# A hybrid decoder layer in one kernel: memory tiles turned later, waits per tile, and sample values in two reduced-precision parts

## The reference

```
x = x + o @ w_out                                  # end of the mixing stage
h = rmsnorm(x, g_xattn)
m = rmsnorm(mem_prompt, g_mem)                     # 256 memory tokens
k, v = m @ xa_w_k, m @ xa_w_v                      # for the prompt; both are outputs too
q = h @ xa_w_q                                     # 4 heads of 512
prompt:  p = softmax(q k^T / sqrt(512)) over 256 memory tokens;  o = p v
samples: the same with cache_mem_k, cache_mem_v    # a K and a V of 256 x 512 for each of 8 samples x 4 heads
x = x + o @ xa_w_o
h = rmsnorm(x, g_ffn)
x = x + (silu(h @ ffn_w_gate) * (h @ ffn_w_up)) @ ffn_w_down
y = rmsnorm(x, g_final)
```

## Time and profile before

| | |
|---|---|
| median of 3 runs | 1907.69 us (1902.86 to 1907.97) |
| the profiled execution's own time | 1903.32 us |
| its span (first to last instruction) | 1901.6 us |
| mean granted TensorE clock, as a share of full | 0.988 |
| PE busy | 1841.4 us, 97% |
| DVE, ACT, POOL busy | 60%, 41%, 10% |

### The profile page before, as it was taken

The page is one execution under the profiler, slowest core; times in us unless marked ns, Lnnn a source line. Parts: engine busy times, 40 slices in busy tenths (PEclk is TensorE's granted clock), DMA queues, the critical chain, the costliest instruction groups (busy, mean ns, idle before and its releaser), DMA issues.

```text
span 1901.6 us, 34195 instructions
## 1 busy us (share of the span) xinstructions
PE 1841.4 (97%) x13832; PEld 1736.7 (91%) x13832; DVE 1141.9 (60%) x1569; ACT 774.5 (41%) x797; POOL 182.0 (10%) x172
## 2 busy tenths in 40 slices
PE   7999999989999899999999999999999999999996
PEld 5999999987999899888648999999999999999996
DVE  4888447744776567555455656666544566665444
ACT  4554545342353343444442344444333344433332
POOL 1000000002105400000002520000000000000331
PEclk9999999999999999999999999999999999999998
DMA  7555545442235557887683668887455889984552
GB/s 214 178 175 175 177 139 170 144 137 99 89 110 186 192 182 244 283 300 249 233 285 112 204 197 252 247 246 217 135 178 179 249 244 249 251 227 136 182 181 76
DMA packets 414225, 367.08 MB, mean 193 GB/s; under 512 B 11391, under 2 KB 373886, under 8 KB 413334
## 3 DMA queue, kind: packets, MB, share of 16 engines
q1 hardware_dynamic: 386456, 340.69, 58.2%
q10 hardware_dynamic: 27694, 25.33, 4.2%
HBM read 347.84 MB, written 18.35 MB: 193 GB/s over the span
## 4 chain that ended last, share of the span: by engine, by line
PE 90%; DVE 5%; ACT 2%; issue 1%; DMA 0%; DVEq 0%; POOL 0%; ACTq 0%; POOLq 0%
PE ps L458 63%; PE ps L534 9%; PE ps L515 4%; DVE w_lo L439 2%; PE ps L936 2%; PE ps L1405 2%; PE ps L501 1%; PE ps L1217 1%; PE ps L1413 1%; PE ps L1232 1%; ACT w_hi L432 1%; PE ps L1135 1%; PE ps L1063 1%; PE ps L1374 1%; PE ps L1143 1%
## 5 line engine op out<-in xcount | busy, mean ns | idle before, releaser
L432 ACT ACTIVATE w_hi<-raw 128x2048 fp32r<-128x2048 f32 (+1 forms) x285 | 512.2, 1797 | 906.9 <-PE ps L458 731.8
L439 DVE TENSOR_TENSOR w_lo<-raw,w_hi 128x2048 fp32r<-128x2048 f32 (+1 forms) x285 | 617.8, 2168 | 289.5 <-ACT w_hi L432 286.6
L458 PE MATMUL ps<-act_hi,w_lo 128*128 128x264 f32 x2560 | 734.3, 287 | 5.7 <-DVE w_lo L439 3.6
L458 PE MATMUL ps<-act_lo,w_hi 128*128 128x264 f32 x2560 | 726.7, 284 | 0.0
L458 PE MATMUL ps<-act_hi,w_hi 128*128 128x264 f32 x2560 | 726.3, 284 | 0.0
L458 PEld LDWEIGHTS ps<-act_hi,w_lo 128*128 128x128 f32 x2560 | 483.8, 189 | 9.6 <-DVE w_lo L439 3.6
L458 PEld LDWEIGHTS ps<-act_lo,w_hi 128*128 128x128 f32 x2560 | 484.0, 189 | 0.4
L458 PEld LDWEIGHTS ps<-act_hi,w_hi 128*128 128x128 f32 x2560 | 481.4, 188 | 0.0
L458 PE MATMUL ps<-ff_hi,w_lo 128*128 128x264 f32 x704 | 200.3, 285 | 0.0
L458 PE MATMUL ps<-ff_hi,w_hi 128*128 128x264 f32 x704 | 200.0, 284 | 0.0
L458 PE MATMUL ps<-ff_lo,w_hi 128*128 128x264 f32 x704 | 199.4, 283 | 0.0
(11 more groups left out here) (417 smaller groups left out, 2155.6 us busy)
## 6 DMA issues: line engine op xcount, KB each, us to landing
raw<-in_w_in_dram SPq DMA_DIRECT2D x56, 1024.0 KB, 7.5
raw<-in_ffn_w_gate_dram SPq DMA_DIRECT2D x44, 1024.0 KB, 5.8
raw<-in_ffn_w_up_dram SPq DMA_DIRECT2D x44, 1024.0 KB, 5.9
raw<-in_ffn_w_down_dram SPq DMA_DIRECT2D x32, 768.0 KB, 4.8
raw<-in_ffn_w_down_dram SPq DMA_DIRECT2D x32, 640.0 KB, 6.0
raw<-in_w_out_dram SPq DMA_DIRECT2D x16, 1024.0 KB, 6.2
raw<-in_xa_w_q_dram SPq DMA_DIRECT2D x16, 1024.0 KB, 7.3
raw<-in_xa_w_k_dram SPq DMA_DIRECT2D x16, 1024.0 KB, 6.9
```

Of the source, the lines that this page charges most:

```text
L432: act.activation(w_part(ph, w_hi[b]), raw_part(ph, r, half), ACT.Copy)\
L439: dve.tensor_tensor(w_part(ph, w_lo[b]), raw_part(ph, r, half), w_part(ph, w_hi[b]), ALU.subtract)\
L458: mm = pe.matmul(ps[:, acc(ph, u), 0:ph.cols], w[b][:, k, :], v[:, kk + k, 0:ph.cols], start=first and k == 0 and m == 0, stop=last and k ...
```

## The change

It has four parts. (1) POOL copies the first two `mt` slices ahead of `squares(2)`, and TensorE does x_q's unit 0 ahead of the first turn. (2) `products` gets a callback before each weight tile; at x_q's and gu0's unit 0 it waits for tiles 13, 14, 15 of `act` one by one, and the waits for all tiles ahead of gu0 and gu1 are gone. (3) Values 0 to 17 are summed by TensorE as two fp32r matmuls (rounded part and remainder): ACT writes the rounded part (`high_values`), DVE the remainder (`low_values`). (4) The split of x_o's second unit comes after value 19 and 20 on ACT and DVE, `keep_rows(3, 1)` after values 16 and 17, and the samples' rows are turned and split one step earlier, with x_o's first unit waiting for the last prompt step only at its last weight tile.

```diff
+HALVED = 18
...
+            pool.wait_ge(mrows_landed, 16)
+            for b in range(2):
+                W(pool, "m_turned", b + 1)
+                pool.tensor_copy(mt[b], mrows[:, :, b * P:(b + 1) * P]).then_inc(mt_ready, 1)
             squares(2, taken(PH["w_out"]), x, TT)
...
-            pool.wait_ge(mrows_landed, 16)
-            with pool.Fori(0, KT // 2) as i:
+            with pool.Fori(1, KT // 2) as i:
...
                 b, h = n // XH, n % XH
-                pe.wait_ge(v_mixed, n + 1)
                 at = NB * XH - 1 - (NB * h + b)
-                pe.matmul(ps[0:NB * XH, 6, :], window[:, at:at + NB * XH], piece_at(NB * XH + n)[0][:, 0, :],
+                if n < HALVED:
+                    pe.wait_ge(v_mixed, n + 1)
+                    r = ring_r[(NB * XH + n - EARLY_PIECES) % RING]
+                    pe.matmul(ps[0:NB * XH, 6, :], window[:, at:at + NB * XH], r[:, 0, :], start=n == 0, stop=False)
+                    pe.matmul(ps[0:NB * XH, 6, :], window[:, at:at + NB * XH], r[:, 1, :], start=False, stop=False)\
+                      .then_inc(N["s_o"], 1)
+                    return
+                pe.wait_ge(v_summed, n + 1)
...
+            def x_taken_to(ph):
+                def ready(k):
+                    if k >= 13:
+                        pe.wait_ge(acc_free, ph.t0 - KT + k + 1 + ACC_CREDIT)
+                return ready
             for n in range(3 * KT):
                 if n < KT:
+                    if n == 0:
+                        products(pe, ph, i, u, act_hi, act_lo, ready=x_taken_to(ph))
                     pe.wait_ge(m_taken, n + 1)
                     pe.wait_ge(mt_ready, n + 1)
...
-                    products(pe, ph, i, u, act_hi, act_lo)
                     if n == 0:
                         sum_squares(2, TT)
+                    else:
+                        products(pe, ph, i, u, act_hi, act_lo)
...
             for j in range(KT):
+                if j == KT - 1:
+                    pe.wait_ge(rows_copied, 3)
+                    for d in range(4):
+                        mm = turn(ps[:, 7, d * 32:(d + 1) * 32], orow[:, d * P:(d + 1) * P])
+                    mm.then_inc(rows_turned, 1)
                 prompt_values(j)
...
-                pe.wait_ge(acc_free, ph.t0 + ACC_CREDIT)
                 for u in range(4):
-                    products(pe, ph, 0, u, act_hi, act_lo)
+                    products(pe, ph, 0, u, act_hi, act_lo, ready=x_taken_to(ph) if half == 0 and u == 0 else None)
...
+            def high_values(n):
+                act.wait_ge(v_summed, n + 1)
+                r = (NB * XH + n - EARLY_PIECES) % RING
+                act.activation(ring_r[r][:, 1, :], ring[r][:, 0, :], ACT.Copy).then_inc(v_halved, 1)
...
+            def low_values(n):
+                dve.wait_ge(v_halved, n + 1)
+                r = (NB * XH + n - EARLY_PIECES) % RING
+                dve.tensor_tensor(ring_r[r][:, 0, :], ring[r][:, 0, :], ring_r[r][:, 1, :], ALU.subtract).then_inc(v_mixed, 1)
...
             for n in range(3 * KT):
-                split(*unit_at(n + 2))
+                if n < 3 * KT - 1:
+                    split(*unit_at(n + 2))
...
                         first_values(2 * (n - 39) + v)
+                    for v in range(2):
+                        high_values(2 * (n - 39) + v)
+                if n == 3 * KT - 1:
+                    keep_rows(3, 1)
             for v in range(18, NB * XH):
+                if v == 20:
+                    split(*unit_at(3 * KT + 1))
                 first_values(v)
...
                 if j < 14:
                     second_values(18 + j)
+                if j == 2:
+                    split(*unit_at(3 * KT + 1))
+                if j == KT - 1:
+                    dve.wait_ge(rows_turned, 1)
```

More of the change, by code:

```diff
@@ L126, in build @@
         rstd = place("rstd", [P, TT], F32)
+        SQ0 = Here.at
         sq = place("sq", [P, 2, TT], F32)
@@ L251, in build @@
         p_s = sq[0:NB * XH, 1, 0:NM]
-        window = sq[:, 0, 5 * NB * XH:7 * NB * XH - 1]
+        window = place("window", [P, 2 * NB * XH - 1], R32, SQ0 + 20 * NB * XH)
+        ring_r = [place(f"ring_r{b}", [P, 2, XD], R32, A0 + 4096 * b) for b in range(RING)]
         orow = place("orow", [NB * XH, XD], F32, Q0 + 4 * KT * TT + 4 * (KT // XH * NM - XD))
@@ L317, in build @@
         v_mixed = sem("v_mixed")
+        v_halved = sem("v_halved")
+        v_summed = sem("v_summed")
         rows_copied = sem("rows_copied")
@@ L443, in mixed_unit, with products @@
             return PH["r" if n < 8 else "z"], n % 8 // 4, n % 4
-        def products(pe, ph, i, u, hi, lo, k0=0, middle=None):
+        def products(pe, ph, i, u, hi, lo, k0=0, middle=None, ready=None):
             b, n = (ph.u0 + u) % 2, ph.u0 + 4 * i + u
@@ L456, in products @@
             for k in range(ph.k):
+                if ready is not None:
+                    ready(k)
                 for m, (w, v) in enumerate(((w_lo, hi), (w_hi, lo), (w_hi, hi))):
@@ L565, in build @@
                      "gdn_sq gdn_sum gdn_ln gdn_normed gdn_turned gdn_ktok gdn_vb gdn_g gdn_gcol gdn_scal "
[L566 removed]
+                     "gdn_pair gdn_dmin gdn_dexp gdn_lt gdn_qkm y_done y_copied tyuy_done inv_ready "
                      "gdn_kbg gdn_f gdn_e gdn_out half_hi half_lo half_done o_mixed bst_landed gdn_sx gdn_sbc gdn_sval "
@@ L926, in _ @@
                     pool.tensor_copy(mt[b], mrows[:, :, ds(i * 2 * P + b * P, P)]).then_inc(mt_ready, 1)
-            pool_link(pool, pool.memset(window, 0.0))
-            pool.memset(window[:, NB * XH - 1:NB * XH], 1.0).then_inc(columns_ready, 1)
+            pool_link(pool, pool.memset(window[:, :].bitcast(F32), 0.0))
+            pool.memset(window[:, NB * XH - 1:NB * XH].bitcast(F32), 1.0).then_inc(columns_ready, 1)
             squares(3, taken(PH["x_o"]), x, TT)
@@ L1402, in sample_values @@
                 b, h = n // XH, n % XH
-                pe.wait_ge(v_mixed, n + 1)
                 at = NB * XH - 1 - (NB * h + b)
-                pe.matmul(ps[0:NB * XH, 6, :], window[:, at:at + NB * XH], piece_at(NB * XH + n)[0][:, 0, :],
+                if n < HALVED:
[6 more added lines that the diff above has]
+                pe.wait_ge(v_summed, n + 1)
+                pe.matmul(ps[0:NB * XH, 6, :], window[:, at:at + NB * XH].bitcast(F32), piece_at(NB * XH + n)[0][:, 0, :],
                           start=n == 0, stop=n == NB * XH - 1).then_inc(N["s_o"], 1)
@@ L1459, in _, with values_kept @@
                     sample_values(18 + j)
-            pe.wait_ge(rows_copied, 3)
-            for d in range(4):
-                mm = turn(ps[:, 7, d * 32:(d + 1) * 32], orow[:, d * P:(d + 1) * P])
-            mm.then_inc(rows_turned, 1)
+            def values_kept(k):
+                if k == KT - 1:
+                    W(pe, "att_oe", KT)
             W(pe, "s_oe", 1)
-            phase_pe(pe, PH["x_o"], ow_hi, ow_lo)
+            ph = PH["x_o"]
+            for u in range(4):
+                products(pe, ph, 0, u, ow_hi, ow_lo, ready=values_kept if u == 0 else None)
+            with pe.Fori(1, ph.loops) as i:
+                for u in range(4):
+                    products(pe, ph, i, u, ow_hi, ow_lo)
             for half in range(2):
                 ph = PH[f"gu{half}"]
-                pe.wait_ge(acc_free, ph.t0 + ACC_CREDIT)
                 for u in range(4):
-                    products(pe, ph, 0, u, act_hi, act_lo)
+                    products(pe, ph, 0, u, act_hi, act_lo, ready=x_taken_to(ph) if half == 0 and u == 0 else None)
                     if half == 0 and u == 0:
@@ L1906, in _ @@
                     keep_columns((n - 20) // 4)
-                if n >= KT and n % 4 == 3:
+                if n >= KT and n % 4 == 3 and n < 3 * KT - 1:
                     keep_rows(n % KT // 4, n // (2 * KT))
@@ L2487, in _ @@
                     dve.tensor_scalar(p_s, p_s, small[0:32, REC, 12:13], None, ALU.mult).then_inc(N["s_pn"], 1)
-                if n:
+                if 0 < n < 3 * KT - 1:
                     split(*unit_at(n + 2))
@@ L2502, in _, with by_head @@
                         second_values(2 * (n - 39) + v)
+                    for v in range(2):
+                        low_values(2 * (n - 39) + v)
+            def by_head(v):
+                return v.rearrange("p (h d) b -> p h d b", d=4)
             for j in range(KT):
@@ L2505, in _ @@
                     second_values(18 + j)
+                if j == 2:
+                    split(*unit_at(3 * KT + 1))
+                if j == KT - 1:
+                    dve.wait_ge(rows_turned, 1)
+                    src = ps[:, 7, 0:KT * NB].rearrange("p (d h b) -> p h d b", d=4, h=XH)
+                    link(dve.tensor_copy(by_head(ow_hi[:, :, T:TT]), src))
+                    dve.tensor_tensor(by_head(ow_lo[:, :, T:TT]), src, by_head(ow_hi[:, :, T:TT]), ALU.subtract)\
+                       .then_inc(N["s_oe"], 1)
                 W(dve, "att_o", j + 1)
```

9 lines of the change are left out of this document (1 added, 8 removed).

## The result

The changed kernel took 1884.44 us (median of 4 runs, 1881.83 to 1889.15), the kernel before 1905.28 in the same comparison (4 runs, 1902.18 to 1907.97): a ratio of 0.9894, 95% interval 0.9863 to 0.9924, a gain of about 20 us, between 14.5 and 26. The forecast was 1888, within 1883 to 1896. The profiled execution took 1886.84, its span 1885.1, at a mean clock of 0.990.

The account below looks back on a forecast made before the run. TensorE, busy 97% of the span, bounds the kernel. Gains 6.5 + 5.2 + 2.8 + 1.0 + 1.6 + 0.3 = 17.4 give 1885.9 from the profiled run, 1890.3 from the median; forecast 1888, range 1883 to 1896.

Parts of the forecast that it names:

- x_q's start: Between w_out and x_q: POOL's part and the turn leave the way, first unit 6.07 instead of 7.28; gain 6.5 us.
- Values 0 to 15: Until unit 47 ends: two fp32r matmuls per value cut each group from 7.61 to 6.71; gain 5.2 us.
- PE never idle for more than 0.1: Expected sign in the after profile, 920 to 970 us: groups of 6.7 without longer PE idles.
- the one that the prediction charged to unit 40: PE waits behind unit 40, which has no values ahead and ends before the 7.1 chain; 0.2 us deducted.
- Values 16, 17 and the prompt's values with x_o's start: Behind unit 47: 2.8 us net from values and prompt steps, plus 1.0 from x_o starting earlier.
- the return of the postponed split: In the prompt's loop: the split delays value 21 some 1.6 and values 18 and 19 another 0.3; cost 2.0 us.
- gu0, gu1: At both starts: gu0's 1.4 wait for `act_lo` goes, gain 1.6 us; gu1's 0.7 wait shrinks, gain 0.3.
- The value chain: Rival, chance 0.15: the values' chain through ACT and DVE outlasts its lead and lengthens groups; 1891 to 1898 us.
- the clock rival: Rival, chance 0.15: short idles at the values' end drop the clock there too; 1890 to 1891.5 us.
- The slower rival: Rival, chance 0.02: `high_values` waiting for DVE block ACT's next `w_hi`, so units hang on it; 1911 us or more.

Follow-up runs that it names:

- The three kernels without this part: Kernel before with only POOL's tiles copied early, only x_q's unit 0 ahead of the turn, or only values 0 to 17 halved: 1896.22, 1895.42, 1896.85 us.
- The doubled copies: Changed kernel with ACT's copy of each value's high half issued twice in the groups behind units 39 to 47: 1897.8 us, one run.
- the kernel with the values first: Changed kernel with the values' operations on ACT and DVE issued ahead of the same unit's weight split and eviction: 1881.7 us, ratio to before 0.9896.
- 32 values halved: Changed kernel with values 18 to 31 also split into two fp32r parts, in the prompt's loop: 1893.9 us, one run.

## Why the prediction was right

**x_q's start** (6.5, measured 6.53). The start 0.06 behind `act_lo`, the unit of 6.07 and the full clock came as read from gu0, and the turn took 0.22 for the 0.25. (The 0.5 from which the 0.25 was halved is in no row: to the unit's first record before it is 0.32, to its row in the chain 0.67.) What the prediction did not see is that either of the two edits would do.

**Values 0 to 15** (5.2, measured 5.5). The matmul with 32 columns costs 0.233, as taken. The chain was sized at 7.1 and measured 7.10, its added operations 0.65 and 0.68 for 0.67 and 0.60. The mis-sized term is PE's own group, 6.71 forecast and 6.51 measured: the 5.78 of a unit behind a float32 value holds 0.2 that a unit behind reduced-precision matmuls (5.58) does not. So PE was 0.2 faster a group, and then the chain, which had just fitted in, took 0.16 of that back: 6.67 on average. The 0.04 that is left, six times, is the 0.3 between 5.2 and 5.5. "PE never idle for more than 0.1" was wrong by this: it idles 0.3 in every second group. The wait of 0.96 ahead of value 0 is the one that the prediction charged to unit 40.

**Values 16, 17 and the prompt's values with x_o's start** (2.8 + 1.0, measured 4.6). The idles came where forecast and slightly smaller: 1.41 for 1.6 and 1.21 for 1.5, 0.20 for 0.3. The end of unit 47 to the first prompt step took 3.5 instead of the 3.8, which is 0.3 of the difference. The mis-sized term is the return of the postponed split, 2.0 in the sum: from the first prompt step to value 31 the loop took 29.07, where it took 28.10 with 0.56 of slow clock in it, 1.5 more at the same clock, and moving the split out of the loop won 1.3. x_o's start came as taken: value 31 to x_o's first matmul took 4.74 before and takes 3.60, a gain of 1.1 for the 1.0, and x_o starts 0.07 behind the prompt's last step.

**gu0, gu1** (1.6 and 0.3, measured 1.7 and 0.25). The three kernels without this part take 887.7 to 888.2 from x_o's start to the end, the kernel before 887.9, the changed one 885.6: 2.2. All kernels that have this part lie at 885.6 to 886.2; but all of them also have x_o's first unit started early, so no run shows this part by itself.

**The rivals.** The value chain did take over, but by 0.3 in every second group, not by the 0.5 in each that the rival stood for. (That 0.5 was itself too high: with both added operations at 0.9, the steps of the prediction give 5.0 + 3 x 0.9 = 7.7, so d is 0.6 and a group 0.3 longer.) The clock stayed up: it is 1.00 in every window from 640 to 1860, and the clock rival fell. The doubled copies show that it was not far off: there the clock fell behind 0.54, 2.06 and 0.53, all shorter than the 3.2 of before. "TensorE: Matmul & The Clock Gate" of the Trainium skill, section "A second HAM failure mode: psum-queue depth-cycling", says that frequent short idles between groups of matmuls can make the clock swing; the doubled copies fit that, and the changed kernel's idles of 1.41, 0.20 and 1.21, at 1.00, show that it need not come so. The slower rival fell: it named ACT not being free as the deciding point, and the doubled copies reached that point at a group of 7.30, still under 7.61.

**The level.** The forecast of 1888 came from the stages (1885.9 against the profiled 1903.32) and 2 us added for the median. The sum of stages was 1.2 too small. The changed kernel's own profile, 1886.84, lies 0.9 above 1885.9, because its w_out began 2.4 later than before, a part that the change does not touch. That the median came 3.6 below 1888 is then 1.2 of stages and otherwise scatter of that kind, as far as the profiles tell; that it came no farther off is in part luck.

## What to carry to other kernels

When two edits remove the same wait, run each alone: here either gave all of it, while the waits per tile at x_q did nothing until one old wait for the whole phase was deleted. When an edit makes the bound engine cheaper by handing work to two others, write down their chain against the lead it has, with (chain + 6.25) / 2 here, the 6.25 being the last value and the next unit, for a lead of one unit (shown at a chain of 7.10), and stop at the stage where the others bind (2.84 against 2.04 a step here). And where unchanged code ahead of the change scatters by more than the change is worth, compare from a landmark behind it.

## What was not expected of the hardware

The same TensorE program reached w_out between 570.3 and 579.5 us in 14 profiles, while the two profiles of the changed kernel agree to 0.1 behind it. 5.8 us of this scatter are there by the 100th matmul, the rest comes in stretches of low clock of different length (0.92 against 1.00 from 300 to 330); what sets either stays open. Of idles and the clock: idles of 1.41, 0.20 and 1.21 left it at 1.00, and so did 1.9 in the kernel with the values first, and 1.41, 1.59, 1.31 and 2.34 within 11 us with 32 values halved; 0.54, 2.06 and 0.53, behind eight groups with 0.5 idle in each, were followed by 0.50, the lower of its levels (1.2 GHz), and so were single idles of 3.2, 3.5, 5.5 and 6.3. So the length of one idle alone does not say whether the clock falls. Two whole float32 values cost their 1.83 and 0.2 more in the row of the unit behind them (5.78, against 5.58 behind halved ones), which showed only when they were gone. By PE's records half of it stands at each change between the types: the first product behind a float32 value is followed after 0.34 instead of 0.23, and the last product ahead of one after 0.33 instead of 0.23.
